# Base blocks of a triangular inverse solved along the free axis on VectorE, softmax exponentials and scaling on ScalarE

## Chip, cores, metric

One core of one Trainium2 chip runs the whole layer. The metric is the device time of one execution in microseconds (us).

## What is computed

One hybrid layer over 4096 tokens and 1024 columns: a pre-norm and one input projection, then two head groups side by side, an output projection, a post-norm and the residual. Group A (4 heads of 128) is a gated delta rule in chunks of 64 tokens, and it needs, for each head and chunk, the solution of a unit lower triangular system of size 64. Group B (8 heads of 64, 2 key heads) is softmax attention over two chunks with a sink. Both are touched by the change:

```
lower = where(strict, einsum('bhnid,bhnjd->bhnij', k_beta, kc) * decay, 0.0)
sol = triangular_solve(eye + lower, rhs, left_side=True, lower=True, unit_diagonal=True)
value, k_cum = sol[..., :d], sol[..., d:]
...
scores = einsum('bnqhgd,bnkhd->bnhgqk', qc, kw) * (SW_HEAD_DIM ** -0.5)
sink = broadcast_to(sinks..., scores.shape[:-1] + (1,))
p = softmax(concatenate([scores, sink], axis=-1), axis=-1)[..., :-1]
out = einsum('bnhgqk,bnkhd->bnqhgd', p, vw)
```

## The kernel before

The tokens are taken in 32 tiles of 128 (two chunks). `run_steps` runs 33 steps on each engine; step t does the projection of tile t and the mixing of tile m = t - 1, so step 0 only projects and step 32 only mixes. Every engine has its own instruction list, written out by hand, and semaphores join them (`done(engine, event, tile)`); nothing is reordered by a scheduler.

On TensorE the projection is cut into 26 pieces, `PIECES`, and `fill(n)` (line 391) issues the next n of them wherever the mixing of tile m would wait for another engine: for each tile ZA (4 pieces), V (4), KVB (2), QB (4), K (4), ZB (4), Q (4). Pieces at line 406 are 24 matmuls of 128 columns; at line 413, 12 of 264 (KVB) or 6 of 512 (QB). f16 pairs (high and low half) carry the projection; the mixing is in f32.

The mixing of a tile, in TensorE's order: transposes of k and v, gram matrices (line 421), rotated q and k, the scores of group B (543), then the inverse, woven together with group B.

The inverse of I + M, for four heads at once, is built by doubling. `inv_u` starts as the inverse of 2 x 2 blocks (lines 1031 and 1034 on VectorE, transposed on TensorE at 530, packed by ScalarE at 747 into `t_buf`). A level lv joins blocks of size 2^lv: `level_p` multiplies the odd part of M with the even inverses (438) and transposes the odd inverses (443); VectorE masks the product (`couple`, 979) while ScalarE copies (`copy_u`, 715 and 716); `level_t` multiplies again (461); VectorE subtracts (`update`, 986). Levels 1 to 5 go so, level 6 (447, 451, 468) gives the inverse of size 64. P4 in the text is `level_p(4)`, T4 is `level_t(4)`. `pack_m` on GpSimd (POOL, 1301) packs the odd part of M for each level. All of `level_p(1)` to `level_t(3)` stands between the scores and the products with v (576).

Softmax of group B: row maxima from PSUM (1062), the sinks' maximum (1066, 1068), the subtraction of the maxima (1071) on VectorE; one exponential over 1024 columns on ScalarE (759); the row sums (1082), the sink's term, reciprocal and factor (1084 to 1088) on VectorE; the scaling by that factor on POOL (1320). TensorE transposes the result (564), ScalarE copies it back (768, 769).

Other names that the prediction uses. On VectorE: `convolve` of q, k and v, four taps of four instructions each (894 for tap 0, 896 for the others); `gates`, a chain of 15 small operations woven into them; rhs (1098), which needs ks = k times state (421); out gating (1108). On ScalarE: `conv_fill` copies a projection piece into `conv_in` (665 to 668), `small_fill` the KVB piece (693 to 699), 779 the QB piece. On POOL: the rotation of k (1285 to 1330) and of q (1285 to 1338), and `post`, the residual addition into `y_out` for the tile before (1359). The queue of SP issues the loads and stores: x_in (next tile's x), rot_tab, y_out (residual), out.

Of the kernel before, what the change touches and what calls it, by code (L numbers as in the profile page):

```python
# [39 lines left out]
LEVELS = 7  # L40
GATE_LINKS = 15
NEG = -1e30
# [32 lines left out]
def build(nc, x, pre_norm_w, w_in, conv_w, dn_a_log, dn_dt_bias, dn_out_norm_w, sw_sinks, w_out,  # L75
# [8 lines left out]
    with ExitStack() as ctx:  # L84
# [76 lines left out]
        ident, upper, neg = c32[:, 0, :], c32[:, 1, :], c32[:, 2, :]  # L161
        rows = x_in[0:57, 0:128]
# [4 lines left out]
        def cut(at, n):  # L167
# [61 lines left out]
                (sem("p_turn"), 1, 6), (sem("p_ready"), 1, 6),  # L229
                (sem("tp_turn"), 1, 5), (sem("t_turned"), 1, 6), (sem("t_ready"), 1, 5),  # L230
                (sem("u_ready"), 1, 6), (sem("t_moved"), 1, 5), (sem("m_odd_ready"), 1, 5)))

        mask_turned, mask_link = sem("mask_turned"), sem("mask_link")
        c0_ready, u0_ready, u0_blank, u0_turned, t0_ready = (
            sem(n) for n in ("c0_ready", "u0_ready", "u0_blank", "u0_turned", "t0_ready"))
# [29 lines left out]
        def over_heads(ap, h):  # L265

            return ap.unsqueeze(1).broadcast_to([128, h, ap.shape[1]])

# [46 lines left out]
        def _(sp):  # L315
# [27 lines left out]
            def step(t, p, mix, proj, prep):  # L343
                m = t - 1
                if prep:
                    done(sp, xl_ready, t)
                    sp.dma_start(x_in[:, :], x[0, bass.ds((t + 1) * TOK, TOK), :]).then_inc(x_loaded, 16)
# [3 lines left out]
                if mix:  # L351
                    if isinstance(m, int) and m == 0:
                        sp.wait_ge(wo_ready, 1)
                    else:
                        sp.wait_ge(stored, m * 16)
                    sp.dma_start(y_out[:, :], x[0, bass.ds(m * TOK, TOK), :]).then_inc(res_loaded, 16)
                    done(sp, post_ready, m)
                    sp.dma_start(out[0, bass.ds(m * TOK, TOK), :], y_out[:, :]).then_inc(stored, 16)

            run_steps(sp, step)  # L360
            sp.wait_ge(stored, NT * 16)


        @block.tensor
        def _(pe):
# [21 lines left out]
            def step(t, p, mix, proj, prep):  # L387
# [37 lines left out]
                def level_p(lv):  # L425

                    if lv == 1:
                        done(pe, t0_ready, m)
# [3 lines left out]
                    if lv < LEVELS - 1:  # L432
# [8 lines left out]
                        if lv == 1:  # L441
                            done(pe, k_tail_ready, m)
# [83 lines left out]
                done(pe, u0_ready, m)  # L526
                done(pe, u0_blank, m)
                done(pe, q_t_ready, m)
                for h in range(4):
                    last = nc.tensor.transpose(heads(2)[:, h, :], inv_u[:, h, :], ident)  # L530
                last.then_inc(u0_turned, 1)
                done(pe, k_win_ready, m)
                done(pe, at_ready, m)
                fill(1)
# [12 lines left out]
                fill(1)  # L547
# [874 lines left out]
```

## Time and profile before

| | |
|---|---|
| median of 3 runs | 2222.37 us (2222.23 to 2222.47) |
| the profiled execution | 2220.89 us |
| its span | 2219.1 us |
| TensorE matmuls busy | 2089.9 us, 94% |
| VectorE busy | 1655.8 us, 75% |
| ScalarE busy | 772.4 us, 35% |
| POOL busy | 688.4 us, 31% |
| granted TensorE clock, mean | 0.991 |

The span is the time from the first to the last instruction of one profiled execution; some 1.8 us of that execution lie around it. Busy shares are averages over the whole program; the first 92 us are the load and the preparation of the weights, in which TensorE waits.

### The profile page before, as it was taken

The numbers are of one execution on the slowest core, as the hardware profiler recorded it, in microseconds if no ns is written. First come the engines' busy times: TensorE is split into PE (matmuls) and PEld (weight loads), VectorE is DVE, ScalarE is ACT, GpSimd is POOL, SyncE is SP. The second block draws the span as 40 slices with busy tenths as digits, with TensorE's granted clock in tenths as the row PEclk, the third lists the DMA queues.
The fourth block names the chain that finished last, engine by engine and source line by source line (L and its number), as shares of the span: only waits on it lengthen the run. The fifth ranks groups of instructions, "written<-read, shape, count | busy, mean of one in ns | idle before, by whom it ended". The sixth has DMA issues, their size and how long they took to land.

```text
span 2219.1 us, 63767 instructions
## 1 busy us (share of the span) xinstructions
PE 2089.9 (94%) x26854; PEld 1700.3 (77%) x26854; DVE 1655.8 (75%) x4880; ACT 772.4 (35%) x2200; POOL 688.4 (31%) x1035
## 2 busy tenths in 40 slices
PE   0389999999999999999999999999999999999996
PEld 0378778878878877887887788788788778878874
DVE  5887777777777777777777777777777777777773
ACT  0533333333333333333333333333333333333332
POOL 0023333332323333332333323233322323332332
PEclk9999999999999999999999999999999999999997
DMA  7101000010000100000000000001100000001000
GB/s 296 65 22 32 2 31 32 32 31 32 31 2 31 32 31 32 32 29 4 31 32 31 31 31 17 17 32 32 32 31 31 6 27 32 32 31 32 22 2 29
DMA packets 26335, 75.37 MB, mean 34 GB/s; under 512 B 5129, under 2 KB 9538, under 8 KB 25026
## 3 DMA queue, kind: packets, MB, share of 16 engines
q1 hardware_dynamic: 26050, 71.29, 9.4%
q8 instruction: 213, 3.49, 0.6%
q14 instruction: 72, 0.59, 0.1%
HBM read 54.50 MB, written 16.78 MB: 32 GB/s over the span
## 4 chain that ended last, share of the span: by engine, by line
PE 82%; DVE 13%; ACT 2%; issue 1%; DMA 1%; SPq 0%; POOL 0%; POOLq 0%; DVEq 0%; ACTq 0%
PE bank L406 31%; PE bank L608 15%; PE bank L413 12%; PE bank L421 9%; DVE qkv L896 4%; PE bank L461 2%; PE bank L438 2%; PE bank L576 2%; PE bank L443 1%; PE bank L543 1%; DVE qkv L894 1%; PE bank L564 1%; DVE w_raw L1242 1%; PE bank L384 1%; DVE small L935 1%
## 5 line engine op out<-in xcount | busy, mean ns | idle before, releaser
L406 PE MATMUL bank<-xt_half,w_raw 128*128 128x128 f16 x15360 | 933.0, 219 | 54.5 <-DVE w_raw L1242 53.9
L406 PEld LDWEIGHTS bank<-xt_half,w_raw 128*128 128x128 f16 x15360 | 890.8, 98 | 66.9 <-DVE w_raw L1242 54.1
L896 DVE SCALAR_TENSOR_TENSOR qkv<-conv_in,cols,qkv 128x128 f32<-128x128 f32 x1152 | 436.4, 421 | 3.5
L413 PE MATMUL bank<-w_raw,xt_half 128*128 128x264 f16 (+1 forms) x1536 | 283.7, 328 | 1.0
L1301 POOL TENSOR_TENSOR cw<-mt,small 128x128 f32<-128x128 f32 x320 | 135.1, 446 | 344.7 <-PE bank L438 321.1
L413 PEld LDWEIGHTS bank<-w_raw,xt_half 128*128 128x128 f16 x1536 | 144.3, 99 | 84.3 <-DVE w_raw L911 8.3
L715 ACT ACTIVATE work<-bank 128x128 f32<-128x128 f32 x160 | 44.4, 277 | 372.3 <-PE bank L443 372.3
L608 PE MATMUL bank<-w_o,inv_t 128*128 128x512 f16 x768 | 171.0, 379 | 2.1 <-DVE inv_t L1175 2.1
L608 PE MATMUL bank<-w_o,out_b_half 128*128 128x512 f16 x768 | 171.0, 379 | 0.0
L675 ACT ACTIVATE tanh_c<-qkv 128x512 f32<-128x512 f32 x96 | 60.5, 630 | 281.5 <-DVE qkv L896 281.5
L1349 POOL TENSOR_TENSOR small<-small 128x1 f32<-128x1 f32 x32 | 6.2, 193 | 435.2 <-ACT work L815 435.2
L608 PEld LDWEIGHTS bank<-w_o,inv_t 128*128 128x128 f16 x768 | 73.9, 98 | 85.3 <-DVE inv_t L1175 2.4
L608 PEld LDWEIGHTS bank<-w_o,out_b_half 128*128 128x128 f16 x768 | 74.0, 98 | 83.0
L911 DVE SCALAR_TENSOR_TENSOR w_raw<-tanh_z,bank 128x512 f32<-128x512 f32 x64 | 43.6, 682 | 107.2 <-ACT tanh_z L684 107.2
L1343 POOL TENSOR_TENSOR small<-small 128x4 f32<-128x4 f32 x32 | 33.8, 1056 | 243.4 <-DVE small L1158 243.4
L979 DVE TENSOR_TENSOR work<-bank,masks 128x64 f32<-128x64 f32 x320 | 55.2, 213 | 61.6 <-PE bank L438 57.8
L1170 DVE TENSOR_TENSOR bank<-bank,w_raw 128x512 f32<-128x512 f32 x32 | 22.4, 699 | 99.1 <-PE bank L622 99.1
L894 DVE TENSOR_SCALAR qkv<-conv_in,cols 128x128 f32<-128x128 f32 x384 | 90.6, 279 | 5.1 <-ACT halo L668 1.6
L905 DVE SCALAR_TENSOR_TENSOR qkv<-tanh_c,qkv 128x512 f32<-128x512 f32 x96 | 66.1, 688 | 34.1 <-ACT tanh_c L675 34.1
L986 DVE TENSOR_TENSOR inv_t<-inv_t,bank 128x64 f32<-128x64 f32 x320 | 54.8, 210 | 48.3 <-PE bank L461 48.2
L1359 POOL TENSOR_TENSOR y_out<-y_out,shared 128x1024 f32<-128x1024 f32 x32 | 75.4, 2357 | 30.7 <-DVE shared L1192 30.7
L1285 POOL TENSOR_TENSOR q_rot<-shared,rot_tab 128x512 f32<-128x512 f32 x32 | 40.7, 1271 | 128.1 <-ACT shared L779 128.1
(215 smaller groups left out, 3575.4 us busy)
## 6 DMA issues: line engine op xcount, KB each, us to landing
x_in<-in_x_dram SPq DMA_DIRECT2D x32, 512.0 KB, 4.7
y_out<-in_x_dram SPq DMA_DIRECT2D x32, 512.0 KB, 4.0
out_dram<-y_out SPq DMA_DIRECT2D x32, 512.0 KB, 2.9
w_raw<-in_w_in_dram SPq DMA_DIRECT2D x8, 1024.0 KB, 13.5
w_o<-in_w_out_dram SPq DMA_DIRECT2D x8, 512.0 KB, 13.4
w_raw<-in_w_in_dram SPq DMA_DIRECT2D x8, 384.0 KB, 12.4
w_raw<-in_w_in_dram SPq DMA_DIRECT2D x8, 256.0 KB, 13.2
rot_tab<-in_rotary_dram SPq DMA_DIRECT2D x32, 64.0 KB, 4.2
```

Of the source, the lines that this page charges most:

```text
L406: last = mm(dst[:, 128 * b:128 * b + 128], w_half[:, c, ws, col:col + 128], xt_half[:, xs, c, :], start=(c == 0 and ws + xs == 0), stop=(c ...
L413: last = mm(dst[:, 0:n_col], xt_half[:, xs, c, :], w_half[:, c, ws, col:col + n_col], start=(c == 0 and ws + xs == 0), stop=(c == NC - 1 a ...
L421: last = mm(bank[b][:, 128 * h:128 * h + 128], lhs[:, h, :], right[:, h, :] if len(right.shape) == 3 else right, start=start, stop=stop)
L608: last = mm(bank[4 + n][:, :], src[:, xs, i, :], w_out_half(c)[:, ws, 512 * n:512 * n + 512], start=(begin and i == 0 and xs + ws == 0), s ...
L675: f(tanh_c[:, :], qkv[:, 4 * g:4 * g + 4, :].rearrange("p h n -> p (h n)"), ACT.Tanh, scale=0.5).then_inc(tanh_c_ready[g], 1)
L894: last = v.tensor_scalar(dst, conv_in[:, b, 0:TOK], tap, None, ALU.mult)
L896: last = v.scalar_tensor_tensor(dst, conv_in[:, b, i:i + TOK], tap, dst, ALU.mult, ALU.add)
L905: v.scalar_tensor_tensor(y, tanh_c[:, :], 1.0, y, ALU.add, ALU.mult).then_inc(qkv_ready[g], 1)
L979: last = v.tensor_tensor(below[:, 64 * r:64 * r + 64], bank[2 + r][:, 0:64], masks[:, lv, 0:64], ALU.mult)
L986: last = v.tensor_tensor(next_columns(lv, 0, 2 * pair, 2 * pair + 2), columns(t_even(lv)[:, 64 * pair:64 * pair + 64], lv), columns(bank[2 ...
L1301: last = g.tensor_tensor(m_odd[lv % 2][:, 128 * r:128 * r + 128].rearrange("p (h b r) -> p h b r", h=4, r=2 ** lv), odd[:, :, :, 1, :], on ...
L1359: g.tensor_tensor(y_out[:, :], y_out[:, :], shared[:, :], ALU.add).then_inc(post_ready, 1)
```

## The change

The inverse now starts from blocks of 16 x 16 (`BASE = 4`), and levels 1 to 3 are gone on every engine. The diagonal blocks of M are masked out and folded to 16 columns a head (`m_near`), written to a DRAM scratch of 32 KB, and read back so that each partition holds the whole block of its rows, 16 x 4 x 16 values, 512 KB in all, in the buffer of x (`m_block`). VectorE then eliminates column after column, 15 times a product and a subtraction, each waiting for the one before, on 60 down to 4 columns. Two last products put the inverse into `t_buf` for P4.

```diff
+        m_block = x_in[:, 0:BLOCK * 4 * BLOCK].rearrange("p (j h n) -> p j h n", j=BLOCK, h=4)
...
+        base_inv = sb("base_inv", [128, 4, BLOCK])
+        near_dram = nc.dram_tensor("near_scratch", (128, 4 * BLOCK), F32, kind="Internal").ap()
...
+                if mix:
+                    done(sp, near_ready, m)
+                    done(sp, xl_ready, t if proj else m)
+                    sp.dma_start(near_dram, m_near.rearrange("p h n -> p (h n)")).then_inc(near_stored, 16)
+                    sp.wait_ge(near_stored, (m + 1) * 16)
+                    sp.dma_start(x_in[:, 0:BLOCK * 4 * BLOCK],
+                                 near_dram.rearrange("(b j) n -> b (j n)", j=BLOCK).unsqueeze(1).broadcast_to(
+                                     [128 // BLOCK, BLOCK, 4 * BLOCK * BLOCK])).then_inc(block_loaded, 16)
...
-                    v.tensor_tensor(halves(prod, 0, 1), halves(mt[:, :, :], 0, 1),
-                                    mask_halves(masks[:, 0, :], 0, 1), ALU.mult).then_inc(c0_ready, 1)
-                    done(dve, c0_ready, m)
-                    v.tensor_tensor(halves(inv_u, 0, 1), mask_halves(ident, 0, 1),
-                                    halves(prod, 0, 1), ALU.subtract).then_inc(u0_ready, 1)
+                    v.tensor_tensor(prod, mt[:, :, :], over_heads(same_base, 4), ALU.mult).then_inc(near_made, 1)
+                    done(dve, near_masked, m)
+                    v.tensor_reduce(m_near, prod.rearrange("p h (b n) -> p h n b", n=BLOCK), AX_X, ALU.add).then_inc(
+                        near_made, 1)
...
+            def invert_base(m):
...
+                dve.wait_ge(block_loaded, (m + 1) * 16)
+                done(dve, base_set, m)
+                for k in range(BLOCK - 1, 0, -1):
+                    if count:
+                        linked()
+                    link(v.tensor_tensor(x_prod[:, :, 0:k], m_block[:, 0:k, :, k].rearrange("p j h -> p h j"),
+                                         base_inv[:, :, k:k + 1].broadcast_to([128, 4, k]), ALU.mult))
+                    yield
+                    linked()
+                    link(v.tensor_tensor(base_inv[:, :, 0:k], base_inv[:, :, 0:k], x_prod[:, :, 0:k], ALU.subtract))
+                    yield
...
-                    v.tensor_tensor(sink_arg, sinks8, row_max, ALU.subtract)
-                    done(dve, post_ready, m - 1)
-                    for half in range(2):
-                        last = v.tensor_tensor(soft[:, 4 * half:4 * half + 4, :], heads(4 + half),
-                                               bc(row_max[:, 4 * half:4 * half + 4], 128), ALU.subtract)
-                    last.then_inc(sub_ready, 1)
-                    update(1)
+                    v.tensor_tensor(sink_arg, sinks8, row_max, ALU.subtract).then_inc(soft_link, 1)
+                    dve.wait_ge(soft_link, m * 5 + 3)
+                    v.tensor_scalar(row_max, row_max, -DH_B ** -0.5, None, ALU.mult).then_inc(sub_ready, 1)
...
-                    f(soft[:, :, :], soft[:, :, :], ACT.Exp, scale=DH_B ** -0.5).then_inc(exp_ready, 1)
-                    copy_u(2)
+                    for hh in range(8):
+                        last = f(soft[:, hh, :], heads(4 + hh // 4)[:, hh % 4, :], ACT.Exp, scale=DH_B ** -0.5,
+                                 bias=row_max[:, hh:hh + 1], accum_out=row_sum[:, hh:hh + 1])
+                    last.then_inc(exp_ready, 1)
...
-                    copy_u(3)
+                    done(act, rsum_ready, m)
+                    for hh in range(8):
+                        last = f(soft[:, hh, :], soft[:, hh, :], ACT.Identity, scale=row_sum[:, hh:hh + 1])
+                    last.then_inc(soft_ready, 1)
...
-                    done(pool, rsum_ready, m)
-                    g.tensor_tensor(soft[:, :, :], soft[:, :, :], bc(row_sum, 128), ALU.mult).then_inc(soft_ready, 1)
```

The softmax is now: exponentials head by head from PSUM with the maximum as bias and the row sum accumulated, and the scaling head by head, both on ScalarE. On POOL, `key_norm` comes first, then the base inverse is set to the unit blocks once the mask product is made (`base_set`), and only then `post(m - 1)`; of `pack_m` the calls for levels 4 and 5 are left, back to back.

On TensorE, from the scores (543 before, 568 now) to the products with v, before:

```order
L413 MATMUL bank<-w_raw,xt_half 128x264 [waits gate_a_ready]
L413 MATMUL bank<-w_raw,xt_half 128x264 x11
L438 MATMUL bank<-inv_t,cw 64x64 [waits m_odd_ready,t0_ready]
L438 MATMUL bank<-inv_t,cw 64x64 x3
L443 MATMUL bank<-c,inv_t 128x128 [waits k_tail_ready]
L413 MATMUL bank<-w_raw,xt_half 128x264 x12
L461 MATMUL bank<-work 64x64 [waits u_ready,p_ready]
L461 MATMUL bank<-work 64x64 x3
L413 MATMUL bank<-w_raw,xt_half 128x512 [waits conv_in_ready2]
L413 MATMUL bank<-w_raw,xt_half 128x512 x5
```

and now, from the same point, to P4 (469):

```order
L437 MATMUL bank<-xt_half,w_raw 128x128 x24
L444 MATMUL bank<-w_raw,xt_half 128x264 [waits gate_a_ready]
L444 MATMUL bank<-w_raw,xt_half 128x264 x11
L452 MATMUL bank<-state,qkv 128x128 [waits vn_ready]
L452 MATMUL bank<-state,qkv 128x128 x3
L444 MATMUL bank<-w_raw,xt_half 128x264 x12
L444 MATMUL bank<-w_raw,xt_half 128x512 [waits conv_in_ready2]
L444 MATMUL bank<-w_raw,xt_half 128x512 x17
L581 MATMUL bank<-c,shared 128x128 [waits soft_ready]
L581 MATMUL bank<-c,shared 128x128 x7
L444 MATMUL bank<-w_raw,xt_half 128x512 x6
L437 MATMUL bank<-xt_half,w_raw 128x128 [waits kv_raw_ready]
```

The small products between the fills are gone, the piece that stood ahead of the scores follows them, and the fills stand in runs of two and four pieces.

On VectorE, from rhs to the update of level 4, before:

```order
L1098 SCALAR_TENSOR_TENSOR rhs<-bank,small,rhs 128x128 x3
L986 TENSOR_TENSOR inv_t<-inv_t,bank 128x4x2x8 [waits tp_turn]
L986 TENSOR_TENSOR inv_t<-inv_t,bank 128x4x2x8
L896 SCALAR_TENSOR_TENSOR qkv<-conv_in,cols,qkv 128x128 [waits conv_link]
L896 SCALAR_TENSOR_TENSOR qkv<-conv_in,cols,qkv 128x128 x3
L979 TENSOR_TENSOR work<-bank,masks 128x64 [waits p_turn]
L979 TENSOR_TENSOR work<-bank,masks 128x64
L1108 TENSOR_TENSOR bank<-bank,w_raw 128x512 [waits y_ready,pv_ready]
L986 TENSOR_TENSOR inv_t<-inv_t,bank 128x2x2x16 [waits tp_turn]
```

and now, from the last link of the inversion:

```order
L1003 TENSOR_TENSOR base_inv<-base_inv,masks 128x4 [waits base_made]
L1009 TENSOR_TENSOR inv_t<-base_inv,masks 128x128 [waits base_made]
L911 SCALAR_TENSOR_TENSOR qkv<-conv_in,cols,qkv 128x128 [waits conv_link]
...
L1140 SCALAR_TENSOR_TENSOR rhs<-bank,small,rhs 128x128 [waits ks_ready]
L1140 SCALAR_TENSOR_TENSOR rhs<-bank,small,rhs 128x128 x3
L1026 TENSOR_TENSOR work<-bank,masks 128x64 [waits p_turn]
L1026 TENSOR_TENSOR work<-bank,masks 128x64
L911 SCALAR_TENSOR_TENSOR qkv<-conv_in,cols,qkv 128x128 [waits conv_link]
L911 SCALAR_TENSOR_TENSOR qkv<-conv_in,cols,qkv 128x128 x3
L1149 TENSOR_TENSOR bank<-bank,w_raw 128x512 [waits y_ready,pv_ready]
L1033 TENSOR_TENSOR inv_t<-inv_t,bank 128x2x2x16 [waits tp_turn]
```

Tap 1 of the convolution of v, and the first gate operations, now follow the inversion, and `couple(4)` (1026) stands ahead of tap 2 instead of behind it.

The queue of SP in one step, now:

```order
L366 DMA near_scratch<-masks 128x64 [waits xl_ready,near_made]
L368 DMA x_in<-near_scratch 128x1x1024 [waits near_stored]
L373 DMA rot_tab<-in_rotary_dram 128x128 [waits q_rot_ready]
L379 DMA out_dram<-y_out 128x1024 [waits post_ready]
L381 DMA y_out<-in_x_dram 128x1024 [waits stored]
L387 DMA x_in<-in_x_dram 128x1024 [waits base_made]
```

Before, the load of x_in stood first and waited for `xl_ready` alone, then came rot_tab, y_out and out.

## Rows read from the trace of the kernel before

**Rows 1.** Busy time in a stretch: length; sum and count by engine; PEclk, DMA share, GB/s.
```profile
1000.00:1066.00 66.00, 65.69 (x858) 53.60 (x855) 49.06 (x150) 23.91 (x73) 21.52 (x32) 1.00 0.09 27
```

**Rows 2.** TensorE's timeline, one tile and the next P4: start, us, line, operation, count.
```profile
996.43 2.84 PE L406 MATMUL bank<-xt_half,w_raw 128*128 128x128 f16 x48
999.11 0.61 PE L530 MATMUL bank<-c,work 128*128 128x128 f32 x4
999.55 1.50 PE L406 MATMUL bank<-xt_half,w_raw 128*128 128x128 f16 x24
1000.99 1.10 PE L543 MATMUL bank<-k_win,q_rot 64*64 64x128 f32 x32
1002.12 1.52 PE L413 MATMUL bank<-w_raw,xt_half 128*128 128x264 f16 x12
1003.58 0.34 PE L438 MATMUL bank<-inv_t,cw 64*64 64x64 f32 x8
...
1005.74 1.47 PE L413 MATMUL bank<-w_raw,xt_half 128*128 128x512 f16 x6
1007.14 0.34 PE L438 MATMUL bank<-inv_t,cw 64*64 64x64 f32 x8
...
1007.58 1.06 PE L421 MATMUL bank<-state,qkv 128*128 128x128 f32 x8
1008.47 1.46 PE L413 MATMUL bank<-w_raw,xt_half 128*128 128x512 f16 x6
...
1011.97 1.04 PE L564 MATMUL bank<-c,shared 128*128 128x128 f32 x8
...
1015.96 0.44 PE L576 MATMUL bank<-shared,v_win 128*64 128x128 f32 x4
...
1016.98 0.34 PE L438 MATMUL bank<-inv_t,cw 64*64 64x64 f32 x8
...
1082.05 0.34 PE L438 MATMUL bank<-inv_t,cw 64*64 64x64 f32 x8
```

**Rows 3.** VectorE's timeline in the same tile.
```profile
991.22 1.83 DVE L1013 TENSOR_SCALAR small<-small 128x4 f32<-128x4 f32 x1
...
994.77 0.43 DVE L1031 TENSOR_TENSOR work<-mt,masks 128x256 f32<-128x256 f32 x1
...
1015.04 1.13 DVE L896 SCALAR_TENSOR_TENSOR qkv<-conv_in,cols,qkv 128x128 f32<-128x128 f32 x4
```

**Rows 4.** Groups by line: count, busy us, mean ns of one, idle us before them.
```profile
L1068 DVE TENSOR_TENSOR small<-small 128x8 f32<-128x8 f32 x32 | 10.1, 314 | 1.1
...
L1084 DVE TENSOR_TENSOR small<-small 128x8 f32<-128x8 f32 x32 | 5.4, 168 | 1.1
```

**Rows 5.** ScalarE's timeline: the squares with sums, and one conv_fill.
```profile
1034.28 0.31 ACT L800 ACTIVATE work<-mt 128x128 f32<-128x128 f32 x1 [1.88 <-DVE mt L1148]
...
1034.59 0.29 ACT L800 ACTIVATE work<-mt 128x128 f32<-128x128 f32 x1
...
1044.67 0.21 ACT L665 ACTIVATE conv_in<-halo 128x12 f32<-128x12 f32 x1 [1.49 <-PE bank L406]
...
1045.40 0.18 ACT L668 ACTIVATE halo<-bank 128x12 f32<-128x12 f32 x1
```

**Rows 6.** POOL's timeline in the same tile.
```profile
990.67 2.35 POOL L1359 TENSOR_TENSOR y_out<-y_out,shared 128x1024 f32<-128x1024 f32 x1 [0.94 <-DVE shared L1192]
...
1012.76 0.50 POOL L1285 TENSOR_TENSOR k_rot<-k_raw,rot_tab 128x128 f32<-128x128 f32 x1
...
1018.75 1.27 POOL L1285 TENSOR_TENSOR q_rot<-shared,rot_tab 128x512 f32<-128x512 f32 x1 [3.99 <-ACT shared L779]
...
1021.52 1.27 POOL L1338 TENSOR_TENSOR q_rot<-q_rot,shared 128x512 f32<-128x512 f32 x1
```

**Rows 7.** DMA issues in that tile: size, median us from issue to landing.
```profile
out_dram<-y_out SPq DMA_DIRECT2D x1, 512.0 KB, 2.9
...
y_out<-in_x_dram SPq DMA_DIRECT2D x1, 512.0 KB, 3.7
```

More of the change, by code:

```diff
@@ L565, in step @@
                 last.then_inc(soft_turned, 1)
-                fill(1)
-                level_t(3)
-                fill(1)
+                fill(2)
                 done(pe, soft_t_ready, m)
                 done(pe, v_win_ready, m)
+                done(pe, k_tail_ready, m)
                 for kv in range(2):
@@ L741, in step @@
                     f(k_win[:, :, 64:192], heads(3)[:, 0:2, :], ACT.Copy).then_inc(k_win_ready, 1)
-                    done(act, u0_turned, m)
-                    for r in range(2):
-                        rows_ = slice(64 * r, 64 * r + 64)
-                        split = heads(2)[rows_, :, rows_].rearrange("p h (q s r) -> p s h q r", s=2, r=2)
-                        for which in range(2):
-                            last = f(t_buf[0][rows_, 128 * which:128 * which + 128].rearrange(
-                                "p (h q r) -> p h q r", h=4, r=2), split[:, which, :, :, :], ACT.Copy)
-                    last.then_inc(t0_ready, 1)
                 if proj:
@@ L844, in _ @@
             dve.wait_ge(mask_link, LEVELS - 1)
[L845 to L846 removed]
+            for lv in range(BASE, LEVELS - 1):
+                v.tensor_tensor(fold[lv], masks[:, lv, 0:64], masks[:, lv, 64:128], ALU.add)
+            v.tensor_reduce(spot, ident.rearrange("p (b n) -> p n b", n=BLOCK), AX_X, ALU.add).then_inc(mask_link, 1)
+            v.memset(inv_u[64:128, :, 0:64], 0.0)
             v.memset(halo[:, :, :], 0.0)
@@ L1079, in step @@
                 if mix:
-                    couple(2)
+                    inversion = invert_base(m)
+                    for _ in range(8):
+                        next(inversion)
                     done(dve, exp_ready, m)
-                    v.tensor_reduce(row_sum, soft[:, :, :], AX_X, ALU.add).then_inc(soft_link, 1)
-                    dve.wait_ge(soft_link, m * 5 + 3)
                     v.tensor_tensor(row_sum, row_sum, sink_arg, ALU.add).then_inc(soft_link, 1)
+                    next(inversion)
                     dve.wait_ge(soft_link, m * 5 + 4)
                     v.reciprocal(row_max, row_sum).then_inc(soft_link, 1)
+                    next(inversion)
                     dve.wait_ge(soft_link, m * 5 + 5)
                     v.tensor_scalar(row_sum, row_max, out_f, None, ALU.mult).then_inc(rsum_ready, 1)
-                    update(2)
+                    for _ in inversion:
+                        pass
                 if proj:
@@ L1100, in step @@
                     last.then_inc(rhs_ready, 1)
-                    update(3)
+                    couple(4)
                 if proj:
```

108 lines of the change are left out of this document (59 added, 49 removed).

## The prediction

> **What bounds the kernel now.** I read the busy time of a stretch first. In 66 us of the steady middle TensorE (PE) is busy for all but 0.3 us, at a granted clock of 1.00, while VectorE (DVE) has 49 us of work [rows 1]. Then PE's timeline: the pieces of one tile follow each other without an idle note, and P4, the products of level 4, starts in this tile at 1016.98 and of the next at 1082.05 [rows 2]. So a tile costs 65.07 us, and it costs what PE's instruction list costs. The list runs 31 times in this form: steps 1 to 31 have both projection and mixing; the last mix has no projection. What leaves PE's list is gained, as long as nobody makes PE wait.
>
> **What PE loses.** All times below are in the tile of rows 2. Four transposes of the first inverse take 0.44 (999.11 to 999.55). Each level below 4 has a P (0.44, as 1007.14 to 1007.58) and a T of four small products (0.28, by difference). Three levels and the transposes: 0.44 + 3 x (0.44 + 0.28) = 2.6 us. Besides, fills that stood alone now run together, and a fill costs 0.1 us less when it follows another (24 matmuls alone 1.44, in a row of 48 half of 2.68). Laid out from 999.11: scores 1.13, fills V3 and KVB0 1.44 + 1.36, ks 0.89, KVB1 1.46 and three QB at 1.30 (alone 1.40), transposes of soft 0.88 (1.04 long against the 1.06 of ks), QB3 and K0 1.39 + 1.34, the products with v 1.02 [rows 2]. The sum is 14.8, so P4 could start at 1013.89 instead of 1016.98: **3.09 us less for each of 31 tiles**, 95.8 us. This holds only if three deadlines are kept, and the rest of this part is about them.
>
> **Deadline 1, the scaled softmax at 1009.3.** Scores are complete at 1000.2; two reductions and three small operations on DVE bring the negated maxima to 1002.2. ScalarE (ACT) first has conv_fill V, which starts when V3 ends (1001.74) and takes 0.91 (L665 to the end of L668, rows 5). Then eight exponentials with sums: four such pairs start 0.30 apart [rows 5], so 8 x 0.30 = 2.4 and they end at 1005.3. DVE needs 0.6 more in between other work, the factors are there at 1006.3, ACT's eight scalings at 0.2 (by the spacing of its shortest instructions; 0.3 at most) end at 1008.1 to 1008.9. Kept by 0.4 to 1.2. The 1.9 us of scaling on POOL and DVE's subtraction and sum go.
>
> **Deadline 2, the base inverse at P4, 1013.89.** The masked M and its fold must be made first. Now L1031 starts at 994.77, but L1013 ahead of it, a multiply of four columns, takes 1.83 and ends at 993.05, just when POOL's y_out addition ends (990.67 + 2.35) [rows 3, 6]. The change moves that addition behind the mask, so L1013 should cost about 0.17, and this chain starts 1.6 earlier, at 993.1. Product and fold of 512 columns: L1031 took 0.43 for 256 columns [rows 3] and L1084 0.168 for 8 [rows 4], hence 1.05 ns a column over 0.16, 0.69 each: ready at 994.5. Then the DMA round trip. A 512 KB store lands in 2.9, a 512 KB load in 3.7 [rows 7]; both together, 6.6, bound the 32 KB store and the load from above, and the load alone, 3.7, from below. I take 1.75 for the small store (a store carries 0.5 MB in the last part of its 2.9) and 3.7: 1000.0; the upper end is 1001.1. No load in these rows is one whose source is read 16 times over, so I keep 2 us more for it in the range: 1003.1.
> The Trainium skill, "DMA: Bandwidth & Descriptors", section "Why a DMA increments its semaphore by 16 and not by 1", speaks against this load: the number of engines is the largest up to 16 that divides the slowest dimension of both sides, and the source here has 8 there, so only 8 engines would work. By it the moving part of the load, some 1.3 us on 16 engines, would double and the blocks would be there at 1001.3. No row of before can show it.
> DVE gets to the inversion only after conv V tap 0: ACT is done at 1002.7, four operations cost at most the 1.13 of L896 x4 [rows 3], I take 0.8: 1003.5. The data should be there. There are 30 dependent links of 60 down to 4 columns, 960 in all: 30 x 0.16 + 960 x 1.05 ns = 5.8, and each waits 0.034 for its forerunner (1.1 us over 32 in L1084's row [rows 4]), 1.0 more: **6.8 us**. Eight come first (2.0, to 1005.5), two run between the softmax operations (0.6, to 1006.15), twenty follow (4.4, to 1010.5), the two final products take 0.3 and 0.2.
> POOL gets in the way. L1068 has the form of L1084 but 0.314 for 0.168, where pack_m runs on POOL [rows 4], and L1013 is the stark case. So a DVE instruction with two SBUF inputs waits out a POOL instruction. POOL's k rotation (five instructions, 2.0 us, from 1012.76 before [rows 6]) now starts at 1006.35, as soon as small_fill is done, and lets about one link pass per instruction, five where nearly nine would: 0.8 us lost. The inverse is ready at **1011.6 to 1011.8**, 2.1 ahead of P4.
> The Trainium skill, "SBUF — State Buffer", in "Practical consequences", has the same: a two-SBUF-input DVE instruction contends with a GpSimd instruction that reads SBUF and fully blocks. Without that rule the inverse would be 0.8 earlier, and the second rival below would not exist.
>
> **Deadline 3, the update of level 4 at P5, 1017.49.** This is the tight one. After the inverse DVE does conv V tap 1 (1.06), two gate operations (0.3), rhs (1.06): 1014.2. Then couple(4), which now stands ahead of tap 2: P4's result is there at 1014.3, couple ends 1014.6, the four instructions of tap 2 start from 1014.56 every 0.265, the last at 1015.36. POOL's q rotation starts 1.77 after P4 (1016.98 to 1018.75, rows 2 and 6), so at 1015.66, and lasts 4.04 in four instructions (to 1021.52 + 1.27). All four get through, with 0.3 to spare, 0.4 with the wait at couple. Out gating 0.6 and the update 0.35 then end at 1016.6, 0.9 before P5. From there the pattern against PE is that of before.
>
> **What costs nothing.** rot_tab's load now stands behind the round trip on SP, about 3 us later, and is wanted at 1006.3; the out store and y_out's load follow POOL's addition at about 996.6 and have until the next tile; x_in's load starts at 1011.8 instead of 993.4 and is wanted some 10 us later. Without that cover each would cost up to its 3.7. The last mix has no fills, so its inversion is bare: it loses at least nothing and saves at most 2.6, or loses at most 6.8 + 0.5 + 0.7; I take 0. Setup gains a few small DVE operations beside the weights' load: 0.
>
> **Sum.** 2220.9 (the profiled execution) - 95.8 = 2125.1. The median of the runs stands 1.5 above that execution, so 2126.6; I say **2127**.
>
> **The rivals.**
> *All deadlines kept*: 0.58, 2127. For it: each price comes from a row of the same engine. Against it: 0.4 us of slack at tap 2 after a chain of 30 links, of which 0.015 each would eat it.
> *Tap 2 partly caught by the q rotation*: 0.24. If the inverse is 0.4 to 1.15 us later than worked out, the fourth instruction of tap 2 meets POOL's first instruction (1015.66 to 1016.93), and with more delay the third and second too, each then waiting for the end of one POOL instruction of 1.27 or 0.73. The update comes at 1018.0, 1018.7 or 1019.4, PE waits 0.5, 1.2 or 1.9 at P5, and 2.6 to 1.2 us a tile stay: 2142 to 2185. The same if small waits of 1 us arise elsewhere.
> *Slower: tap 2 wholly caught*: 0.14 in all for no gain or a loss. Beyond 1.15 us of delay all four instructions meet all four of POOL's, tap 2 ends at 1019.9, the update at 1020.8 and PE waits 3.3: the gain is gone (2228). If the inverse is 3.5 late (blocks landing at 1007, or links at 0.34 instead of 0.23), P4 itself waits until 1015.1, the rotation runs to 1020.9, the update comes at 1022, 4.5 behind its time: 1.5 a tile worse than now, 2269. For it: no load of this kind is in the trace; against it: 3 us of slack in the DMA. The page's rule on engines takes 1.3 of them; without it I would give 0.11.
> *The work does not leave PE's path*: 0.04. If DVE became the bound: 49 + 4 us of work against 62 speaks against it. It would give about half, 2175.
>
> **Range and chances.** From 2118 (a tile also sheds 0.27 of wait at T6) to 2185, the end of the second case. A measurement of this kernel can tell about 0.2%, 4 us. Faster by more: 0.85; within: 0.03; slower: 0.12.
>
> **What would show it.** PE's period 62.0 between two P4; no wait at the transposes of soft, P4, T4 or P5. The first link at 1003.5 in this tile's frame, blocks landed earlier, links 0.16 to 0.22 long, L1013's successor near 0.2, the last base product near 1011.8. If tap 2's instructions show 1 us and end with POOL's q rotation, the second rival holds; if the first link waits for a DMA, the third. Idle notes at P4 naming DVE would make the forecast wrong outright.

## The result, and the profile after

| | before | after |
|---|---|---|
| median | 2222.3 us (2221.4 to 2222.5) | **2138.5 us** (2136.7 to 2140.7) |
| profiled execution / its span | 2220.9 / 2219.1 us | 2140.7 / 2138.8 us |
| TensorE (PE) busy | 94% | 93% |
| VectorE (DVE) busy | 75% | 78% |
| ScalarE (ACT) busy | 35% | 39% |
| POOL busy | 31% | 25% |

The ratio is 0.9623, 95% interval 0.9611 to 0.9635: **3.8% faster**, inside the range, 11.5 us above the predicted 2127. The middle stretch, as [rows 1]:

```profile
1220.00:1286.00 66.00, 65.73 (x851) 54.99 (x840) 52.46 (x180) 27.26 (x93) 16.48 (x25) 1.00 0.16 47
```

Behind the length stand PE, its weight load, DVE, ACT and POOL. PE has as little idle time as before; DVE has 52.5 of 66 us where it had 49.1. P5 and T6 below are to levels 5 and 6 what P4 and T4 are to level 4. PE's timeline in one normal tile, to the next P4, as [rows 2]:

```profile
1281.13 1.10 PE L568 MATMUL bank<-k_win,q_rot 64*64 64x128 f32 x32
...
1285.76 5.40 PE L444 MATMUL bank<-w_raw,xt_half 128*128 128x264 f16 x30
1290.99 1.04 PE L581 MATMUL bank<-c,shared 128*128 128x128 f32 x8
...
1295.62 0.34 PE L469 MATMUL bank<-inv_t,cw 64*64 64x64 f32 x8
...
1299.21 0.34 PE L469 MATMUL bank<-inv_t,cw 64*64 64x64 f32 x8
...
1305.24 0.45 PE L499 MATMUL bank<-work 64*64 64x64 f32 x8 [0.28 <-DVE work L1023]
...
1357.40 0.34 PE L469 MATMUL bank<-inv_t,cw 64*64 64x64 f32 x8
```

P4 to P4 is 61.78 us where it was 65.07: 3.29 less. From the scores to P4 it is 14.49, where the prediction laid out 14.78. The only wait left in a normal tile is 0.28 at T6, 499. To compare with the times of the prediction, which are those of another tile (its frame), take 282.02 from the times of this one.

DVE's timeline in the same tile, as [rows 3]:

```profile
1275.05 0.69 DVE L1078 TENSOR_TENSOR work<-mt,masks 128x512 f32<-128x512 f32 x1
1275.78 1.02 DVE L1080 TENSOR_REDUCE masks<-work 128x64 f32<-128x512 f32 x1
...
1285.45 0.25 DVE L999 TENSOR_TENSOR masks<-x_in,base_inv 128x60 f32<-128x60 f32 x1
1285.74 0.22 DVE L1003 TENSOR_TENSOR base_inv<-base_inv,masks 128x60 f32<-128x60 f32 x1
...
1287.56 0.17 DVE L1125 TENSOR_TENSOR small<-small 128x8 f32<-128x8 f32 x1
...
1289.43 0.49 DVE L999 TENSOR_TENSOR masks<-x_in,base_inv 128x32 f32<-128x32 f32 x1
...
1293.36 0.49 DVE L1009 TENSOR_TENSOR inv_t<-base_inv,masks 128x128 f32<-128x128 f32 x2
1293.77 1.14 DVE L911 SCALAR_TENSOR_TENSOR qkv<-conv_in,cols,qkv 128x128 f32<-128x128 f32 x4
...
1296.39 1.13 DVE L911 SCALAR_TENSOR_TENSOR qkv<-conv_in,cols,qkv 128x128 f32<-128x128 f32 x4
1297.43 0.69 DVE L1149 TENSOR_TENSOR bank<-bank,w_raw 128x512 f32<-128x512 f32 x1
1298.04 0.35 DVE L1033 TENSOR_TENSOR inv_t<-inv_t,bank 128x64 f32<-128x64 f32 x2
...
1300.47 1.10 DVE L911 SCALAR_TENSOR_TENSOR qkv<-conv_in,cols,qkv 128x128 f32<-128x128 f32 x1
```

The first link starts in the frame at 1003.4 (predicted 1003.5), the base products end at 1011.7 (1011.6 to 1011.8), tap 2 starts at 1014.4 (1014.56) and is not stretched. The link of 0.49 lies beside POOL's rotation of k. POOL's rotation of q follows tap 2 (its three rows are four instructions), and stretches the single tap instructions behind it, as the 1.10, and a gate operation of four columns that takes 0.16 where no rotation runs beside it (experiments 5 to 9):

```profile
1298.73 0.68 DVE L950 TENSOR_SCALAR small<-small 128x4 f32<-128x4 f32 x1
...
1297.39 1.27 POOL L1326 TENSOR_TENSOR q_rot<-shared,rot_tab 128x512 f32<-128x512 f32 x1 [7.10 <-ACT shared L792]
1298.62 1.45 POOL L1328 TENSOR_TENSOR shared<-shared,rot_tab 128x256 f32<-128x256 f32 x2
1300.15 1.27 POOL L1373 TENSOR_TENSOR q_rot<-q_rot,shared 128x512 f32<-128x512 f32 x1
```

So the normal tile ran as forecast. But 31 x 3.29 is 102 us, and the spans differ by 80.3. Taken from scores to scores:

- 29 tiles at 3.29 less: -95.4, but seven of them are longer than 61.78, by 10.2 together (4.16, 2.59, 1.24 and four of 0.4 to 0.7): -85.2
- the first tile with mixing, 64.98 before, 67.91 now: +2.9
- the step behind, whose projection is the last, 59.42 to 58.01: -1.4
- the last step, 52.56 to 55.29: +2.7; ahead of the first scores: +0.55 (no finding: in the profiles of this document they start anywhere from 153.8 to 155.8)

The worst of the seven begins at 1153.42. SP's issues in the normal tile, then in this one:

```profile
1276.83 0.33 SPq L366 DMA_DIRECT2D near_scratch<-masks  x1
1278.28 0.60 SPq L368 DMA_DIRECT2D x_in<-near_scratch  x1
...
1149.12 0.33 SPq L366 DMA_DIRECT2D near_scratch<-masks  x1
1152.72 0.60 SPq L368 DMA_DIRECT2D x_in<-near_scratch  x1
```

and what DVE and PE waited for in it:

```profile
1159.79 0.26 DVE L999 TENSOR_TENSOR masks<-x_in,base_inv 128x60 f32<-128x60 f32 x1 [1.96 <-DMA x_in<-near_scratch]
...
1165.72 1.09 PE L581 MATMUL bank<-c,shared 128*128 128x128 f32 x8 [2.28 <-ACT shared L778]
```

The small store normally lets the load be issued 1.45 after it, here 3.60. **The load then takes 7.07**, from its issue to the first link (1152.72 to 1159.79). In a normal tile that means a landing at about 1285.35, just when DVE comes (1285.45): there is no slack in the DMA at all. DVE stands still, and behind the first eight links on its queue are the three operations for the softmax factors (1125 to 1131), so ACT's scaling (778) is late and PE waits at the transposes of soft. The DMA arrives at deadline 1 before it arrives at deadline 2.

PE's wait explains 2.3 of the 4.16 us. The rest is in its granted clock, which is the first of the three values at the end of a row (before the DMA share and GB/s); the first two rows are of this tile, the third of the tile from 1466.47, whose wait was 2.37:

```profile
1165.42:1168.42 3.00, 2.69 (x13) 1.57 (x14) 2.65 (x14) 1.34 (x3) 0.00 (x0) 0.75 0.00 0
1168.42:1171.42 3.00, 3.00 (x32) 2.54 (x32) 1.91 (x9) 0.21 (x1) 0.00 (x0) 0.68 0.49 175
...
1481.47:1484.47 3.00, 3.00 (x55) 2.65 (x52) 2.52 (x12) 0.49 (x3) 0.00 (x0) 1.00 0.55 175
```

A clock of 0.68 over 3 us, with 0.75 in the 3 us before, means that for a part of them the lower of the two levels, 1.2 GHz, was granted: 0.32 x 3 + 0.25 x 3 = 1.7 us of work lost. The other tile kept 2.4 GHz and is 1.6 us shorter with the same wait. In the first mixing tile, too, the clock falls (0.51 at 170.75) after a wait of 4.22.

Why is the store late? In the DMA view, the stretch 1148 to 1153.5 shows, beside the 144 packets of the store, one of another queue, and so does the late tile at 1461 to 1467:

```profile
q1 hardware_dynamic: 144, 0.03, 3.0%
q8 instruction: 1, 0.02, 1.0%
```

In the normal tile, 1276 to 1279, the second row is missing. Over the 31 tiles that follow one another, the 4.4 us ahead of 0.5 us before the scores hold such an instruction fetch in 15: all seven late tiles, the first one, and seven that are not late. None of the 16 tiles without it is late. In six of the late tiles it is the store that takes longer; in the seventh (from 1091.24) the store takes its 1.46, and DVE's chain ahead of it runs 0.3 to 0.4 later. That the fetch delays the store is inferred; no run isolates it.

### The profile page after: what moved, and what is told of

It is laid out like the page before. It is cut to its first block, busy times and chain, and to the rows that moved or that the text cites. A ratio compares the mean times of both kernels' runs of the same rounds, so it can differ in the third digit from the quotient of the medians.

```text
span 2138.8 us, 60953 instructions
## 1 busy us (share of the span) xinstructions
PE 1990.7 (93%) x25094; PEld 1649.5 (77%) x25094; DVE 1670.1 (78%) x5459; ACT 836.7 (39%) x2616; POOL 527.7 (25%) x811
## 4 chain that ended last, share of the span: by engine, by line
PE 57%; DVE 30%; DMA 5%; ACT 5%; issue 3%; SPq 0%; POOL 0%; POOLq 0%; DVEq 0%; ACTq 0%
PE bank L437 26%; PE bank L624 15%; PE bank L452 8%; DVE qkv L911 7%; DVE base_inv L1003 4%; DVE masks L999 4%; DMA x_in<-near_scratch 3%; DVE qkv L909 2%; DVE w_raw L1283 1%; ACT conv_in L682 1%; PE bank L415 1%; DVE rhs L1140 1%; PE bank L568 1%; DMA near_scratch<-masks 1%; DVE small L950 1%
## 5 line engine op out<-in xcount | busy, mean ns | idle before, releaser
L911 DVE SCALAR_TENSOR_TENSOR qkv<-conv_in,cols,qkv 128x128 f32<-128x128 f32 x1152 | 394.7, 386 | 3.5
L444 PE MATMUL bank<-w_raw,xt_half 128*128 128x264 f16 (+1 forms) x1536 | 269.6, 329 | 0.0
L444 PEld LDWEIGHTS bank<-w_raw,xt_half 128*128 128x128 f16 x1536 | 149.5, 98 | 87.9 <-issue 1.9
L999 DVE TENSOR_TENSOR masks<-x_in,base_inv 128x60 f32<-128x60 f32 (+14 forms) x480 | 108.4, 226 | 26.3 <-DMA x_in<-near_scratch 13.2
L1003 DVE TENSOR_TENSOR base_inv<-base_inv,masks 128x60 f32<-128x60 f32 (+14 forms) x480 | 106.1, 221 | 15.4
L909 DVE TENSOR_SCALAR qkv<-conv_in,cols 128x128 f32<-128x128 f32 x384 | 91.0, 283 | 18.9 <-ACT halo L684 15.4
L768 ACT ACTIVATE shared<-bank,small 128x128 f32<-128x128 f32 x256 | 89.6, 376 | 0.0
L778 ACT ACTIVATE shared<-shared,small 128x128 f32<-128x128 f32 x256 | 78.2, 388 | 16.0 <-DVE small L1131 16.0
L681 ACT ACTIVATE conv_in<-halo 128x12 f32<-128x12 f32 x96 | 20.1, 209 | 163.7 <-PE bank L437 163.7
L1326 POOL TENSOR_TENSOR k_rot<-k_raw,rot_tab 128x128 f32<-128x128 f32 x32 | 15.0, 470 | 271.0 <-issue 236.2
```

The lines of the kernel that those rows point to most:

```text
L444: last = mm(dst[:, 0:n_col], xt_half[:, xs, c, :], w_half[:, c, ws, col:col + n_col], start=(c == 0 and ws + xs == 0), stop=(c == NC - 1 a ...
L768: last = f(soft[:, hh, :], heads(4 + hh // 4)[:, hh % 4, :], ACT.Exp, scale=DH_B ** -0.5, bias=row_max[:, hh:hh + 1], accum_out=row_sum[:, ...
L778: last = f(soft[:, hh, :], soft[:, hh, :], ACT.Identity, scale=row_sum[:, hh:hh + 1])
L909: last = v.tensor_scalar(dst, conv_in[:, b, 0:TOK], tap, None, ALU.mult)
L911: last = v.scalar_tensor_tensor(dst, conv_in[:, b, i:i + TOK], tap, dst, ALU.mult, ALU.add)
L999: link(v.tensor_tensor(x_prod[:, :, 0:k], m_block[:, 0:k, :, k].rearrange("p j h -> p h j"), base_inv[:, :, k:k + 1].broadcast_to([128, 4, ...
```

## The experiments

**1. The load on more engines.** The scratch holds every block twice, so that the source of the load has 16 rows for its slowest dimension.

```diff
-        near_dram = nc.dram_tensor("near_scratch", (128, 4 * BLOCK), ...
+        near_dram = nc.dram_tensor("near_scratch", (128 // BLOCK, 2, 4 * BLOCK * BLOCK), ...
...
+                    for copy in range(2):
+                        sp.dma_start(near_dram[:, copy, :]..., m_near...).then_inc(near_stored, 16)
...
+                                 near_dram.rearrange("b c n -> (b c) n").unsqueeze(1).broadcast_to([16, 8, ...
```

> The scratch holds every block twice, so that the load's source has 16 as its slowest dimension instead of 8; two 32 KB stores instead of one, and the same 512 KB load. Theory (only 8 DMA engines carry the changed kernel's load, which lands 7.0 us after its issue): with 16 it lands in 4.5 to 5.7, the second store costs about 0.4. Normal tiles keep their period of 61.78, tiles whose store is late wait less at the first link (1.96 becomes under 0.9), the first and the last tile each gain 1 to 1.5: 2125 to 2133 against 2138.5. Rival (the load is slow because 16 partitions read the same 4 KB, whatever the engines): it still lands in about 7.0, the second store makes every tile 0.4 late, the softmax factors and the transposes of soft follow: 2145 to 2155.

2127.1 us (2124.2 to 2129.1), ratio 0.9568 (0.9553 to 0.9582), inside the expected range. The row of the load in the page's list of DMA issues now has a landing time:

```profile
x_in<-near_scratch SPq DMA_DIRECT2D x32, 512.0 KB, 4.7
```

7.0 becomes 4.7, though the store pair takes 2.52 for 1.45, 1.07 more where 0.4 was expected. Every middle tile is 61.77, with one store pair as late as 4.06; the first mixing tile falls from 67.9 to 65.7. The last step did not gain as expected, it takes 56.4 for 55.3 (the step before it 57.0 for 58.0). The late tiles were the load's: with it 1.2 earlier, none is left.

The run changes two things about the load at once: how many engines carry it, and how often each row is read (8 times for 16). The engines can be seen in the DMA share, the busy share of the 16 engines. Just after the load has begun it is, in the change and in this run:

```profile
1279.60:1280.40 0.80, 0.80 (x18) 0.80 (x16) 0.24 (x1) 0.53 (x1) 0.26 (x1) 1.00 0.53 56
...
1269.40:1270.20 0.80, 0.80 (x24) 0.70 (x25) 0.68 (x2) 0.00 (x0) 0.00 (x0) 1.00 1.01 338
```

So about half of the engines work in the one, and all in the other. What the fewer readings of a row add to the gain is not separated.

**2. Tap 1 as cover for the load.** Tap 1 goes back ahead of the inversion, and the softmax factors come after four links.

```diff
+                    if proj:
+                        convolve(t, FILL_V, [1])
                     inversion = invert_base(m)
-                    for _ in range(8):
+                    for _ in range(4):
```

> Tap 1 of the convolution of v moves ahead of the inversion, and the softmax factors come after 4 links instead of 8. Theory (what is lost against 31 x 3.29 us are late blocks: in 7 of 31 tiles the store lands late, DVE stands at the first link, and the softmax factors queued behind it make PE wait at the transposes of soft): DVE reaches the first link 1.06 later, so that much of a late block is covered; normal tiles stay at 61.78, the late ones lose 1 us less each, the first and last tile about 1 less: 2128 to 2134. Rival (the late tiles lose time in the links and POOL's locks, not in the wait): unchanged, 2136 to 2141.

2127.9 us (2126.0 to 2129.1), ratio 0.9572 (0.9556 to 0.9588), 0.1 us below the expected range. The load is as slow as in the change, DVE comes to it 1.2 us later (the first link 5.50 after the scores for 4.32), and no middle tile is late: 61.77 in all. So with the same work on DVE, its order alone removes the late tiles. Two limits: two pieces of the order move at once, and the profiled execution has only three late stores, of 2.66 at most, none of the 3.6 that cost the change most.

**3, 4. The two halves of the change alone.** The new base inverse with the old softmax, and the new softmax with the old levels (with the scaling ahead of `copy_u(3)`):

```diff
-                    for hh in range(8):
-                        last = f(soft[:, hh, :], heads(4 + hh // 4)[:, hh % 4, :], ACT.Exp, ...
+                    f(soft[:, :, :], soft[:, :, :], ACT.Exp, scale=DH_B ** -0.5).then_inc(exp_ready, 1)
...
+                    g.tensor_tensor(soft[:, :, :], soft[:, :, :], bc(row_sum, 128), ALU.mult)...
```

> The base inverse of the change with the softmax of before: subtraction and row sums on DVE, one exponential on ScalarE, scaling on POOL between pack_m(4) and pack_m(5). Theory (DVE and its lock with POOL have no room left in front of P4; the softmax's move is what makes the room): DVE has 2.4 us more ahead of the end of the inversion, POOL's scaling of 1.9 and pack_m(5) lock out two-input links for 2 us more, the inverse comes about 16.5 us after the scores' start where P4 wants it at 14.5, and conv V tap 2 falls into the q rotation: period 65 to 68, 2230 to 2320, no gain over before. Rival (the time is PE's instruction list, the rest is covered): 2138 to 2150.

> The softmax of the change alone (exponentials with bias and sum head by head, scaling on ScalarE ahead of copy_u(3)), with all levels of the inverse as before. Theory (PE's list is unchanged and PE was never waiting there): period 65.07 within 0.1, 2217 to 2226 against 2222.3. Rival (the softmax on ScalarE shortens a chain by itself): below 2215; or ScalarE's 2.5 us more work delays copy_u(2) and copy_u(3): above 2235.

The base inverse alone: 2284.7 us, ratio 1.0278 (1.0263 to 1.0294), **slower**. The softmax alone: 2222.7 us, ratio 1.0000 (0.9990 to 1.0009), nothing. In the view of waits of the first:

```profile
PE bank L469 <- DVE inv_t L1025: 62.4, 31, 2.1
```

PE waits at P5 for 2.06 in 30 tiles (and for 0.46 in the last), besides 0.70 at the transposes of soft, 0.38 at P4 and 0.88 at T4; the tile is 65.91 or 67.44. The old softmax puts a subtraction and a sum on DVE and the scaling on POOL, and the inversion is late for everything behind it. In this order of the queues, removing 3.3 us from PE's list is worth something only with the second half, which by itself is worth nothing: the parts do not add.

**5, 6, 7. How near the cliff is.** One or two reductions of 512 columns whose results nobody uses, ahead of the final products:

```diff
                 assert count == BASE_LINKS
+                for _ in range(2):
+                    v.tensor_reduce(x_prod[:, :, _], prod, AX_X, ALU.max)
```

> One reduction of 512 columns into a spare cell of x_prod (about 0.6 us of DVE, result unused) between the last link and the two final products of the base inverse. In a normal tile of the changed kernel tap 2's fourth instruction starts 0.2 before POOL's q rotation, so: theory (a two-input DVE instruction waits out the POOL instruction that runs): the third and fourth instructions of tap 2 each wait for one, the update of level 4 ends 1.2 after P5's time, PE waits there, period about 63.0, 2165 to 2185. Rival (only DVE's work counts, P4 is 2 us away and the update has 0.9 of slack): period 61.8, 2138 to 2143.

2167.7 us (2166.0 to 2168.3), ratio 0.9747 (0.9731 to 0.9763): 0.6 us of DVE's time costs 1.1 a tile (62.89), as the theory had it. Tap 2 and PE's wait at P5 in one tile:

```profile
1309.93 2.61 DVE L911 SCALAR_TENSOR_TENSOR qkv<-conv_in,cols,qkv 128x128 f32<-128x128 f32 x4
...
1313.46 0.34 PE L469 MATMUL bank<-inv_t,cw 64*64 64x64 f32 x8 [1.25 <-DVE inv_t L1035]
```

> The change, with two 512-column reductions added ahead of the final products on VectorE, their results unused: about 1.2 us of VectorE's time a tile, twice that of e1's sister run with one reduction. Lock theory: all four instructions of tap 2 now start behind GpSimd's rotation of q and wait it out, so that the update of level 4 is over 3 us late at P5; VectorE's wait ahead of tap 2 is about 2.5 us, TensorE's at P5 2.5 to 3.3 us, and the normal tile takes 64.3 to 65.4 us: 2212 to 2250 us, most likely 2235. Rival, only VectorE's own work counts (0.6 us more than with one reduction, whose tile took 62.9): 63.5 us a tile, 2180 to 2192 us.

2224.6 us (2221.9 to 2226.7), ratio 1.0008 (0.9999 to 1.0018): 1.2 us a tile on an engine that is 78% busy, and **the whole gain of 84 us is gone**. The time is in the expected range, the wait at P5 below it (2.06 for 2.5 to 3.3). PE's, DVE's and POOL's timelines in one tile:

```profile
1280.83 0.34 PE L469 MATMUL bank<-inv_t,cw 64*64 64x64 f32 x8 [2.06 <-DVE inv_t L1035]
...
1276.84 3.08 DVE L911 SCALAR_TENSOR_TENSOR qkv<-conv_in,cols,qkv 128x128 f32<-128x128 f32 x4
...
1276.88 1.43 POOL L1328 TENSOR_TENSOR q_rot<-shared,rot_tab 128x512 f32<-128x512 f32 x1 [7.33 <-ACT shared L792]
```

Tap 2 meets the rotation of q and takes 3.08 for 1.13 (2.61 with one reduction). It starts 0.04 us ahead of the rotation, so only its first instruction comes through. The Trainium skill, "SBUF — State Buffer", in "Practical consequences", says that a VectorE instruction with two inputs in SBUF contends with a GpSimd instruction that reads SBUF, and the trace agrees: 3.08 for 1.13. Yet the tile is not 63.8 everywhere: 17 of the 29 middle tiles take 65.3 or more (one of them, 65.85, for a late load). Two stretches 3 us long right behind the wait at P5, in a tile of 63.80 and in one of 65.33:

```profile
1281.41:1284.41 3.00, 3.00 (x57) 2.74 (x54) 2.53 (x14) 2.24 (x7) 0.00 (x0) 1.00 0.00 0
...
1345.21:1348.21 3.00, 3.00 (x37) 2.69 (x35) 1.43 (x11) 1.73 (x5) 0.00 (x0) 0.53 0.02 5
```

After the same wait of 2.06 the clock stays at 1.00 in the one, and at half for some 3 us in the other, which makes the 1.5 us; it fell behind 16 of the 28 waits at P5. So it is in experiment 3 (65.91 and 67.44). Behind the waits of 1.25 (one reduction) it fell in no middle tile.

> The same two reductions, but ScalarE's copy of the piece that q is rotated from is moved behind the copy of U's last level, so that GpSimd's rotation of q starts some 3.6 us later and tap 2 is issued ahead of it. Lock theory: the rotation no longer holds tap 2; the update is late at P5 only by the two reductions' 1.2 us less the slack of 0.2 to 0.5 there, so that a tile takes 62.5 to 63.2 us: 2150 to 2175 us. Rival, the delay itself and not the rotation costs the time: as e8, within 5 us of it.

The edit moves ACT's copy of the QB piece:

```diff
+                if mix:
+                    copy_u(5)
                 if proj:
                     done(act, fill_ready[FILL_QB], t)
...
-                if mix:
-                    copy_u(5)
```

2225.9 us (2221.8 to 2234.8), ratio 1.0019 (1.0008 to 1.0030): this expectation failed, the time is that of the rival. But not for the rival's reason. Tap 2 takes 1.13 and PE waits for nothing at P5; it waits here:

```profile
1289.64 0.45 PE L499 MATMUL bank<-work 64*64 64x64 f32 x8 [1.68 <-DVE work L1025]
```

The rotation now runs from 1283.98 to 1288.4, on top of tap 0 of conv K, and makes the first of its four operations of 0.28 into 0.74, and two gate operations among them into 0.70 and 1.23; level 6's copies are late, and the clock falls behind this wait in 22 of the 29 middle tiles. To delay the blocking instruction only moved the collision.

**8, 9. The rotation taken away.** From the second tile on, POOL rotates one head of q of eight:

```diff
+                    nq = 1 if mix else 8
-                    rotate(q8, rot_in, rot_sw, 8).then_inc(rot_link, 1)
+                    rotate(q8[:, 0:nq, :], rot_in[:, 0:nq, :], rot_sw[:, 0:nq, :], nq).then_inc(rot_link, 1)
...
-                    g.tensor_tensor(q8, q8, rot_sw, ALU.add).then_inc(q_rot_ready, 1)
+                    g.tensor_tensor(q8[:, 0:nq, :], q8[:, 0:nq, :], rot_sw[:, 0:nq, :], ALU.add).then_inc(q_rot_ready, 1)
```

> The two unused reductions again, and in every tile but the first GpSimd rotates one of the eight heads of q instead of all (the other seven keep the first tile's rotated values), so that its four instructions are short. Theory, the loss of 85 us with two reductions is GpSimd's rotation of q holding VectorE, and what the waits that it makes do to TensorE's clock: tap 2 takes 1.1 to 1.4 us, TensorE waits 0.3 to 0.7 us at P5 for the 1.2 us of delay, the granted clock stays at 1.00 in the middle tiles, and a tile takes 62.0 to 62.5 us: 2143 to 2162 us. Rival, the 1.2 us of VectorE's time cost 2 us of waiting by themselves: above 2200 us.

> The change with the one-head rotation alone, as the control: the rotation of q is on no path in the change, so the tile stays at 61.78 us and the time at 2134 to 2141 us. Rival, the rotation holds something there too: below 2132 us.

With both reductions: **2136.0 us** (2134.8 to 2137.2), a normal tile is 61.92 and the clock is whole in the middle:

```profile
1295.08 1.20 DVE L911 SCALAR_TENSOR_TENSOR qkv<-conv_in,cols,qkv 128x128 f32<-128x128 f32 x4
...
1297.19 0.34 PE L469 MATMUL bank<-inv_t,cw 64*64 64x64 f32 x8 [0.18 <-DVE inv_t L1035]
```

Against experiment 6, 88.6 us are gone: 1.88 a tile by the wait, 1.5 more by the clock in 16 of them, and the late tiles. The theory holds, and the price of the reductions themselves was below my lower end. The control went against me: 2125.4 us (2123.8 to 2126.4), ratio 0.9562 (0.9546 to 0.9578), tile 61.47. The rotation does hold something in the change: the gate operations and taps behind it (the 1.10 above, 0.34 now) start level 6 late, and the 0.28 at T6 is its doing. That is 9 of the control's 13 us; the rest is mostly that its late tiles cost 5.5 us in place of 10.2. Against this control the two reductions cost 10.6 us (0.45 a tile), where with the whole rotation they cost 86.1.

**10, 11. Versions to keep.** Experiments 1 and 2 together, and then the coupling of level 6 ahead of tap 0 of conv K:

```diff
                 if proj:
                     silu(t, 2)
+                if mix:
+                    couple(6)
+                if proj:
                     convolve(t, FILL_K, [0], ks_ready if mix else None, m, gate_steps)
                 if mix:
-                    couple(6)
```

> The 16-engine load and tap 1 ahead of the inversion together. Theory: the blocks are there before DVE in every tile, also with a late store; all middle tiles at 61.78; the first and last tile 1 to 2 better than in e2: 2118 to 2128, faster than the change. Rival (the doubled store delays as much as the load gains): like e2.

> Scratch as two copies, tap 1 ahead of the inversion, and the coupling of level 6 moved ahead of tap 0 of conv K, against the 0.28 us that TensorE waits at T6 in every normal tile. Theory: the wait goes, the tile takes 61.5 to 61.6 us, 2113 to 2119 us. Rival: ScalarE's copy of the inverse ends last there, the tile stays at 61.77, 2121 to 2125 us.

Both together: 2123.0 us (2122.1 to 2125.0), ratio 0.9549 (0.9535 to 0.9563), first mixing tile 63.3. With the coupling moved: **2120.7 us** (2118.9 to 2121.8), ratio 0.9540 (0.9524 to 0.9556); the tile is 61.67, and PE waits at the same place for another:

```profile
1290.22 0.45 PE L501 MATMUL bank<-work 64*64 64x64 f32 x8 [0.17 <-ACT work L729]
```

0.28 less for DVE has become 0.17 for ACT's copy. The tile is 0.1 shorter; the intervals of the two ratios overlap, and the expected 2113 to 2119 was missed, the median by 1.7. It is the fastest version here, 18 us below the change and 102 below the kernel before. (Both are quicker than the control without the rotation: the late tiles and the first mixing tile, 63.3 and 63.2 for its 67.8, weigh more than T6.)

## Why the prediction was right, and where it was not

**PE's list: right.** 3.09 a tile was 3.29. Three stretches were laid out 0.1 too long: the scores 1.04 for 1.13, V3 with KVB0 2.70 for 2.80, KVB1 with three QB 5.23 for 5.36.

**Deadline 1: kept in 22 of 29 tiles, by less than said, and missed in seven.** The exponentials of ACT start 0.34 apart (from 1284.63), not 0.30, and get longer from the first to the last (0.35 to 0.40), so they end at 1005.4 in the frame for 1005.3; the scalings are done at 1008.7 (1288.28 + 2.44), inside what was given. What the prediction did not have is that the factor operations stand on DVE **behind eight links that wait for a DMA**. It counted them as "the factors are there at 1006.3" in one part and counted the DMA's slack in another, against P4. Deadline 1 and deadline 2 were one chain. The prediction named a first link that waits for a DMA as the sign of its third rival, but there PE was to wait at P4; the sign came in seven tiles, and PE waited at the transposes of soft.

**Deadline 2: right sum, wrong terms.** The fold took 1.02 for 0.69: I priced a reduction over strided columns by a product of the same size. The small store 1.45 for 1.75. **The load 7.0 for 3.7**, and that is the step that failed: blocks at 1000.0, or 1003.1 at worst, were in truth at about 1003.3, outside both ends. "The data should be there" came out true by 0.1 us, which was luck; where the store was late as well, it was false. The bound was taken from the plain loads of [rows 7], with 2 us for the pattern that no row showed; the load took 3.3 more. The Trainium skill, "DMA: Bandwidth & Descriptors", section "Why a DMA increments its semaphore by 16 and not by 1", gave eight engines for a source with 8 in its slowest dimension, and I turned it into 1.3 us more. Experiment 1, with 16 there, agrees with the rule: a DMA share of 1.01 for 0.53, and 2.3 us less. Whether the 4.7 that are left hold a price of the pattern stays open: the plain loads have medians of 3.3 in the change, and of 4.0 and 4.7 in the kernel before. The sum came out because the blocks were not late for DVE in a normal tile, and the rest was well priced: from the first link to the end of the last, with the factor operations and the rotation of k in between, it took 7.9; forecast 7.8.

**Deadline 3: right, and right about why it was tight.** Tap 2's last instruction starts 0.2 ahead of the rotation (0.3 forecast). The rule was put too narrowly, for instructions with two inputs in SBUF: operations with one are held too (L950 above, 0.68 for 0.16, and already L1013 before, 1.83). Experiments 5 to 9 show the mechanism and the cliff: the second rival's state has 62.9 a tile, the third's 63.8 and more. The third's price at P5 was forecast as 3.3 and measured as 2.06, since the first instruction of tap 2 still comes through; what brought the loss to the full gain was the clock (24 of the 86 us), which no rival had.

**Costs set at 0.** The last step has no fills, and lost 2.7 where "0, bounds -2.6 and +8" was said: the load is bare there (DVE idle 3.70 ahead of its first link, PE 9.56 at the transposes of soft). The first mixing tile was treated as one of the 31, and it is not: from the fold to the row maxima DVE takes 4.8 us for 6.5, so the load is 2.7 late. The last step with projection gained 1.4, not 3.1.

Against the forecast of 95.8 us: +5.8 (0.2 more in 29 tiles), -10.2 (late tiles), -6.0 (first mixing tile), -1.7, -2.7 and -0.55 (the ends) give 80.4. The three places where DVE waits for the load, 19 us together (late tiles, first mixing tile, last step), are more than the shortfall of 15.4; the better list hid a third of them.

## What to carry to other kernels

Ask of every instruction behind a DMA wait on an in-order queue who waits for it, not only of the result that the DMA is for. A load whose access pattern no row of the trace shows has no upper bound from the plain ones; leave it slack, by its size, its number of rows or a piece of work put ahead of it. Where two engines block each other, the price of a delay is set by what it then collides with: here 1.2 us of it cost 0.45 a tile without the other engine's instruction, and 2.0 to 3.6 with it (experiments 8 and 6).

## What was not expected of the hardware

- A 512 KB load that reads 8 source rows of 4 KB, each 16 times over, took 7.0 us; with 16 rows (8 times over) 4.7; a plain load of 512 KB 3.3 (x_in, y_out, medians of the change; 4.7 and 4.0 before). Transfers queued behind it are late with it: rot_tab lands 6.5 after its issue (4.2 before), the store of out 7.1 (2.9 before).
- A 32 KB store and the wait for it take 1.45 us, but 1.94 to 3.67 in six of the middle tiles of the change, all of them with an instruction fetch of 16 KB in the same few microseconds.
- TensorE's granted clock falls to the lower level for about 3 us after some waits and not after others of the same length: 2.06 us (experiment 6) cost 1.5 more in 16 of 28 middle tiles, 1.68 us (experiment 7) 1.6 more in 22 of 29, and 1.25 us (experiment 5) nothing more in any. A wait ahead of PE had two prices.
- A reduction of 512 columns in fp32 takes 0.68 us over adjacent values, to 4 results, and 1.02 when it reads every 16th, to 64 results; which of the two costs the time is not separated.
- A VectorE operation of 4 columns with one input in SBUF (L950) takes 0.68 us beside GpSimd's rotation and 0.16 without it.
- ACT's exponentials of 128 x 128 with bias and row sum follow each other every 0.34 us.
